# Two more pairs as block products in the second and third networks, and the columns that move with them

## The reference, cut to what matters

```
mod = cond @ mod_w[i] + mod_b[i]                       # 9 x 1024 values a layer
h = modulate(rms_norm(x), sh1, sc1)
x = x + 0.5 * g1 * swiglu(h, ffn1_w_gu[i], ffn1_w_down[i])
h = modulate(rms_norm(x), sh2, sc2);  x = x + g2 * mixer(h)
h = modulate(rms_norm(x), sh3, sc3)
x = x + 0.5 * g3 * swiglu(h, ffn2_w_gu[i], ffn2_w_down[i])
x = rms_norm(x, post_gain[i])
def swiglu(h, w_gu, w_down):
    g, u = jnp.split(h @ w_gu, 2, axis=-1)
    return (jax.nn.silu(g) * u) @ w_down
```

## Time and profile before

| | us |
|---|---|
| median of three runs | 1936.67 |
| the three runs | 1937.36, 1936.67, 1932.82 |
| the profiled execution | 1936.46 |
| its span, first to last instruction | 1934.7 |
| TensorE busy | 1903.3 (98% of the span) |
| VectorE busy | 1508.9 (78%) |
| ScalarE busy | 967.6 (50%) |
| POOL busy | 212.5 (11%) |

### The profile page before, as it was taken

One profiled execution on the slowest core, in us unless ns is written; L12 is line 12 of the kernel. 1 busy time (PEld: TensorE's weight loads), 2 busy tenths in 40 slices (PEclk: granted clock), 3 DMA queues, 4 the chain that ended last, 5 costly groups with the idle time before them and its releaser, 6 DMA issues.

```text
span 1934.7 us, 29256 instructions
## 1 busy us (share of the span) xinstructions
PE 1903.3 (98%) x11364; PEld 1690.3 (87%) x11364; DVE 1508.9 (78%) x2264; ACT 967.6 (50%) x1556; POOL 212.5 (11%) x245
## 2 busy tenths in 40 slices
PE   6999999999999999999999999999999999999998
PEld 5789989888888889899888999977888889899897
DVE  7889888699868798897888988785555478578485
ACT  5324626464746436346542653655565456356264
POOL 3110000016710020000011000001101000000000
PEclk9999999999999999999999999999999999999999
DMA  8775352322053583633267443323223232323232
GB/s 336 275 277 188 123 174 92 119 88 88 23 163 120 187 287 115 224 110 103 80 207 258 164 147 116 109 88 115 88 91 95 61 98 83 125 87 120 77 101 75
DMA packets 76411, 264.84 MB, mean 137 GB/s; under 512 B 8897, under 2 KB 11073, under 8 KB 76274
## 3 DMA queue, kind: packets, MB, share of 16 engines
q1 hardware_dynamic: 55296, 190.34, 30.3%
q0 software_dynamic: 20256, 72.02, 10.8%
q10 hardware_dynamic: 722, 0.61, 0.1%
HBM read 260.66 MB, written 2.13 MB: 136 GB/s over the span
## 4 chain that ended last, share of the span: by engine, by line
PE 88%; DVE 7%; issue 1%; DMA 1%; POOL 1%; ACT 1%; SPq 0%; DVEq 0%; ACTq 0%; POOLq 0%
PE bank L1862 17%; PE bank L1867 16%; PE bank L1863 16%; PE bank L1943 11%; PE bank L1942 11%; PE bank L1944 11%; DVE arena L1679 1%; DVE arena L1215 1%; DVE top L1678 1%; PE bank L2348 1%; PE bank L2365 1%; PE bank L2280 1%; PE bank L2124 1%; DVE h_lo L1395 1%; DVE wlo L1125 1%
## 5 line engine op out<-in xcount | busy, mean ns | idle before, releaser
L1862 PE MATMUL bank<-hid_hi,whi 128*128 128x512 f32 (+1 forms) x856 | 328.8, 384 | 0.0
L1863 PE MATMUL bank<-hid_hi,wlo 128*128 128x512 f32 (+1 forms) x856 | 328.0, 383 | 0.0
L1867 PE MATMUL bank<-hid_lo,whi 128*128 128x512 f32 (+1 forms) x856 | 328.0, 383 | 0.0
L1862 PE MATMUL bank<-h_hi,whi 128*128 128x512 f32 x784 | 313.4, 400 | 5.2 <-ACT h_hi L779 2.8
L1863 PE MATMUL bank<-h_hi,wlo 128*128 128x512 f32 x784 | 307.1, 392 | 0.0
L664 ACT ACTIVATE whi<-wraw 128x1024 fp32r<-128x1024 f32 x210 | 219.4, 1053 | 150.1 <-PE bank L1867 129.6
L1942 PE MATMUL bank<-h_hi,whi 128*128 128x256 f32 x1024 | 289.9, 283 | 0.5 <-ACT sq L724 0.5
L1943 PE MATMUL bank<-h_hi,wlo 128*128 128x256 f32 x1024 | 289.7, 283 | 0.0
L1944 PE MATMUL bank<-h_lo,whi 128*128 128x256 f32 x1024 | 289.7, 283 | 0.0
L1125 DVE TENSOR_TENSOR wlo<-wraw,whi 128x1024 fp32r<-128x1024 f32 x196 | 238.2, 1223 | 58.6 <-ACT whi L664 58.2
L1867 PE MATMUL bank<-h_lo,whi 128*128 128x512 f32 x784 | 279.4, 393 | 3.1 <-POOL h_lo L561 3.0
(11 more groups left out here) (294 smaller groups left out, 3353.7 us busy)
## 6 DMA issues: line engine op xcount, KB each, us to landing
wraw<-in_w_units_dram SPq DMA_DIRECT2D x306, 512.0 KB, 3.8
arena<-in_mod_t_dram POOLq DMA_DIRECT2D x96, 512.0 KB, 5.2
mod_tile<-in_mod_t_dram POOLq DMA_DIRECT2D x32, 512.0 KB, 5.5
wraw<-in_w_units_dram SPq DMA_DIRECT2D x32, 384.0 KB, 3.2
arena<-in_w_units_dram SPq DMA_DIRECT2D x10, 512.0 KB, 4.3
arena<-in_mod_t_dram SPq DMA_DIRECT2D x7, 512.0 KB, 5.9
xT<-in_xt_dram SPq DMA_DIRECT2D x8, 256.0 KB, 4.2
sq<-k_roots POOLq DMA_DIRECT2D x8, 256.0 KB, 3.7
```

The lines of the kernel that those rows point to most:

```text
L1862: pe.matmul(dst, whi[:, w, k, :], hi_, start=first, stop=False)
L1863: pe.matmul(dst, wlo[:, w, k, :], hi_, start=False, stop=False)
L1867: return pe.matmul(dst, whi[:, s % RING, k, :], lo_, start=False, stop=last)
```

## The change

- f = 1 and f = 2 have 4 plain pairs in place of 6, so 18 of 22 pairs are summed in place of 16.
- The three first `split_t` of these networks stand behind pair 1, the fourth behind pair 3; `round_t` accordingly. It is the arrangement that f = 3 has already.
- Columns: f = 1 has 5 in the pairs (2 behind pair 2, 3 behind pair 3; 6 before), 20 in the first down stage as before, 15 in the second (14 before). f = 2 has 4 (1 behind pair 2, 3 behind pair 3; 6 before), 20, and 8 (6 before).
- The post gain of f = 2 stands behind pairs 0, 1 and 2 (1, 3 and 4 operations) in place of 0, 2 and 3.
- `fetch` computes which earlier column must be done from the slot's last use, as the number of columns in the pairs is now 5 or 4.

```
-              [None] * KT + [(0, 0, n) for n in (3, 3, 3, 4, 4, 4)]
+              [None] * KT + [(0, 0, n) for n in (2, 2, 3, 3, 3)]
...
-              + [(1, 1, d) for d in (0, 0, 0, 1, 1, 1, 2, 3, 3, 4, 5, 5, 7, 7)],
+              + [(1, 1, d) for d in (0, 0, 0, 1, 1, 1, 2, 3, 3, 4, 4, 5, 5, 7, 7)],
-              [(0, 0, n) for n in (3, 3, 3, 4, 4, 4)] + [(0, 1, d) for d in (0, 0, 0, 1, 1, 1, 2, 2, 2, 3, 3, 3, 4, 4, 5, 5, 6, 6, 7, 7)]
-              + [(1, 1, d) for d in (0, 0, 0, 1, 1, 1)], []]
+              [(0, 0, n) for n in (2, 3, 3, 3)] + [(0, 1, d) for d in (0, 0, 0, 1, 1, 1, 2, 2, 2, 3, 3, 3, 4, 4, 5, 5, 6, 6, 7, 7)]
+              + [(1, 1, d) for d in (0, 0, 0, 1, 1, 1, 2, 2)], []]
...
-PLAIN_PAIRS = {0: (8, 0, 0), 1: (6, 0, 0), 2: (6, 0, 0), 3: (4, 0, 0)}
+PLAIN_PAIRS = {0: (8, 0, 0), 1: (4, 0, 0), 2: (4, 0, 0), 3: (4, 0, 0)}
...
-            return m % 3 if m < 6 else (m - 6) % 4
+            n = late_three(t)
+            return m % 3 if m < n else (m - n) % 4
+
+        def late_three(t):
+
+            return 4 if t >= FFN_TILES[2] else 5
...
-        T_ROUND_AT = {..., 1: {0: (0, 1, 2), 4: (3,)}, 2: {0: (0, 1, 2), 4: (3,)}, ...}
-        T_SPLIT_AT = {..., 1: {1: (0, 1), 2: (2,), 5: (3,)}, 2: {1: (0, 1), 2: (2,), 5: (3,)}, ...}
-        POSTS_AT = {0: (0,), 2: (1, 2, 3), 3: (4, 5, 6, 7)}
+        T_ROUND_AT = {..., 1: {0: (0, 1, 2), 2: (3,)}, 2: {0: (0, 1, 2), 2: (3,)}, ...}
+        T_SPLIT_AT = {..., 1: {1: (0, 1, 2), 3: (3,)}, 2: {1: (0, 1, 2), 3: (3,)}, ...}
+        POSTS_AT = {0: (0,), 1: (1, 2, 3), 2: (4, 5, 6, 7)}
...
-                m, n = t - late_first(t), 6
+                m, n = t - late_first(t), late_three(t)
...
-                pool.wait_ge(mod_done, max(t - (0 if m == 0 else 2 if 3 <= m < n + 3 else MOD_RING - 1), MOD_FIRST))
-                if m in (0, n + 3):
+                pool.wait_ge(mod_done, max([u + 1 for u in range(late_first(t), t) if late_place(u) == late_place(t)], default=late_first(t))
+                             if t >= FFN_TILES[1] + KT else t - MOD_RING + 1)
+                if t >= FFN_TILES[1] + KT and m in (0, n + 3):
```

More of the change, by code:

```diff
@@ L321, in build @@
         MOVING_SUM = (0, 0, 3, 1, 2, 0, 4)
-        T_ROUND_AT = {0: {0: (0, 1, 2), 6: (3,)}, 1: {0: (0, 1, 2), 4: (3,)}, 2: {0: (0, 1, 2), 4: (3,)}, 3: {0: (0, 1, 2), 2: (3,)}}
-        T_SPLIT_AT = {0: {2: (0, 1, 2), 7: (3,)}, 1: {1: (0, 1), 2: (2,), 5: (3,)}, 2: {1: (0, 1), 2: (2,), 5: (3,)}, 3: {1: (0, 1, 2), 3: (3,)}}
-        POSTS_AT = {0: (0,), 2: (1, 2, 3), 3: (4, 5, 6, 7)}
+        T_ROUND_AT = {0: {0: (0, 1, 2), 6: (3,)}, 1: {0: (0, 1, 2), 2: (3,)}, 2: {0: (0, 1, 2), 2: (3,)}, 3: {0: (0, 1, 2), 2: (3,)}}
+        T_SPLIT_AT = {0: {2: (0, 1, 2), 7: (3,)}, 1: {1: (0, 1, 2), 3: (3,)}, 2: {1: (0, 1, 2), 3: (3,)}, 3: {1: (0, 1, 2), 3: (3,)}}
+        POSTS_AT = {0: (0,), 1: (1, 2, 3), 2: (4, 5, 6, 7)}
         def sum_banks(s):
```

## The result

| | us |
|---|---|
| median after (4 runs, 1946.23 to 1948.56) | 1946.68 |
| median before beside it (4 runs, 1932.82 to 1937.36) | 1935.93 |
| ratio after to before | 1.0067, 95% interval 1.0055 to 1.008 |
| profiled execution after: time, span | 1946.23, 1944.4 |

The changed kernel is slower by 0.55 to 0.80%, clear of the 0.3% that such a measurement can tell. The forecast was 1946.8 us, +10.3 us. The ratio, on 1935.93 us, is +13.0 us (10.6 to 15.5); the two medians of the table are 10.75 us apart, near the lower end of that interval.

A forecast was written before the change was run, and what follows sets the result against it. TensorE was taken as the bound, with 88% of the chain of waits. The terms -3.1 + 3.6 + 8.0 + 0.4 + 1.4 = +10.3 us on the profiled 1936.46 us gave 1946.8 us, range 1940 to 1951.

The forecast's parts named there:

- Saving, 3.1 us: Four pairs of f = 1 and f = 2 turn from plain to summed, each 0.77 us less on TensorE: 3.1 us less.
- The estimate of 4.7 us: Same saving by the skill's matmul price, 10.35 against 9.17 us a pair; the prediction preferred the rows' 3.1 us.
- f = 1, three columns, 3.6 us: Columns behind pair 3 delay `combine` and `three_keep`; TensorE idles 3.6 us at product 6 of the first summed pair.
- f = 1, two columns behind pair 2, 0: Two columns, 2.4 us, fit into VectorE's 2.96 us of idle time in f = 1; cost zero.
- f = 2, post gains, 4.7 us: TensorE wants all eight post gains before f = 2's first summed pair; VectorE finishes late, a new 4.7 us wait.
- f = 2, columns behind it, 3.3 us: Three columns behind pair 3 again stand before `combine`: a second wait of 3.3 us at product 6, after 0.3 credited.
- Second down stage, 0.4 us (0 to 1.5): f = 2's two columns behind unit 2 delay SP's load and the following `combine`: 0.4 us, bounds 0 and 1.5.
- Clock, 1.4 us (0 to 2.8): Granted clock falls after TensorE's long waits; 0 to 2.8 us for f = 1, middle 1.4; f = 2's mostly absorbed.
- columns hidden: Rival: VectorE's slack hides the columns in both networks, leaving only the saving, 1933.4 us; chance 0.10.
- columns alone: Rival: f = 2's post gains are done in time, columns cost 3.6 and 3.6, 1941 to 1942.4 us; chance 0.13.
- late tiles: Rival: first columns land 2 us late in either network and the clock falls fully in both, up to 1952; chance 0.07.
- The room of the tiles: Column fetches in f = 1 land at 623.3, wanted at 623.7; room of 0.4 to 1 us before lateness adds.

The follow-up runs named there:

- the run with moved columns: Changed kernel with the three columns behind pair 3 of f = 1 and f = 2 moved behind summed pairs 3, 4, 5 of the second third; ratio 1.0021.
- the run with TensorE kept busy: Changed kernel with idle 512-column matmuls ahead of the three waits (14 in f = 1; 19 and 12 in f = 2); ratio 1.0048 to the kernel before.
- the run that changes the second network alone: Changed kernel with f = 2 put back to six plain pairs and its old places, so only f = 1 changed; ratio 1.0020 to the kernel before.

## Why the prediction was right, step by step

- *Saving, 3.1 us:* shown where the waits were taken away, 1.62 + 1.57 = 3.2. The pace of the rows held. The estimate of 4.7 us, worked out from the Trainium skill: TensorE: Matmul & The Clock Gate (section "Wait — 56ns, not 53.3ns?"), is not what these stretches show.
- *f = 1, three columns, 3.6 us:* 3.68, by the chain that was named. Moved away, the wait is gone.
- *f = 1, two columns behind pair 2, 0:* right. VectorE was done with them 0.38 us before pair 3.
- *f = 2, post gains, 4.7 us:* 4.69. Left out, the wait is gone.
- *f = 2, columns behind it, 3.3 us:* 2.64 with the slow clock and 3.5 without; right in place, and its size hung on the clock.
- *Second down stage, 0.4 us (0 to 1.5):* 0.36, and 1.1 from start to start in the run with moved columns.
- *Clock, 1.4 us (0 to 2.8):* this term was mis-sized. It cost 4.2 us net, outside its bounds, as the run with TensorE kept busy shows: 1.5 in f = 1, as taken, but 2.7 in f = 2, where I had the slow matmuls eat into the second wait and took nothing. They did so for 0.9 us; 1.2 us came through by `one_keep`, and the second wait brought another fall of the clock behind it, 1.5 us, which the sum did not have. The trace of before already had a fall in the middle of the run (the mixer's, last section), of which the working, with the rows of the start alone, made no use.
- *Left out:* the wait of the earlier trace rows, which the new places of f = 2's columns took away, 0.8 us less.
- *The total:* the sum was about 2 us short of the 12.5 that the stages show and about 3 short of the ratio's 13.0. That the time was met to 0.1 us all the same is luck: the sum stood on an execution of before that was 1.1 + 1.9 = 3.0 us longer than the profiled one of after where nothing was changed. Later runs of before have medians of 1933.42 (19 runs) and 1933.67 us (17 runs), against the 1936.67 that the sum stood beside.
- *The rivals:* columns hidden, columns alone and late tiles did not come about. The room of the tiles was real, though: five columns behind pair 3 ran out of it by 3.0 us.

## What to carry to other kernels

Before work is put "into the idle time" of an engine that is not the bound, see on which side of its next deadline the idle time lies: VectorE's 5.4 us stood ahead of an operation that waited for TensorE, and behind it there was no slack at all. A stage that already runs the planned arrangement without the extra work, as f = 3 did here, gives that deadline to a tenth of a microsecond. And when the gain is a few microseconds, each long wait here also cost the slow matmuls behind it, 1.5 us in f = 1; move the work into a stage whose deadlines are met early, and the small gain appears.

## What was not expected of the hardware

The clock did not always fall during the idle time; where its fall began differed even behind the same wait. In f = 1 of the changed kernel TensorE went on at 636.81 and first ran at its full pace (13 matmuls in the 1.60 us up to 638.40, at a granted clock of 0.98); the row of 638.40 is at 0.50, and that of 641.80 at 1.00 again. Behind the second wait of f = 2 it was the same, with slow matmuls from 1000.1 on. But behind the first wait of f = 2 the matmuls were slow from the first one, at 985.07, and so they were in f = 1 of the run that changes the second network alone, where TensorE had waited the same 3.52 us:

```profile
636.70 0.58 PE L1948 MATMUL bank<-h_hi,whi 128*128 128x256 f32 x1 [3.52 <-ACT sq L730]
636.70:642.20 5.50, 5.50 (x26) 5.50 (x26) 5.50 (x9) 2.31 (x4) 0.00 (x0) 0.50 0.78 264
```

There the half clock lasted 5.5 us in place of 3.2 to 3.4, and that is the 1.0 us by which this run's f = 1 was dearer. In the two networks the clock fell so after waits of 3.5, 4.5 and 2.5 us, the last of which I had not counted on, and not after those of 1.0 us or less. Elsewhere it fell after less: in the mixer of the second layer, the profile of before has a wait of 1.54 us and the granted clock at 0.50 from 1320 to 1322 us behind it; in the profile after, the wait there is 1.20 us and the clock does not fall. Idle matmuls in the wait held it at 1.00.
